# Two transformer-like blocks on one core: opening loads, the token factor of the feed-forward, buffers of the pooled branch, the sums at block two's entry, and a pause of VectorE

## The reference, cut to what matters

```python
h = rmsnorm(x, norm_mix)
q, k, v, r, lr_f, lr_b, u, g_a, g_b = split(h @ w_in)
log_a = log_sigmoid(lr @ w_decay_up + b_decay) / 16      # forward and backward, from 16 columns each
o = gla(q, k, v, log_a_f) + flipped gla(..., log_a_b)    # gated linear attention, 4 heads, chunks of 64
y_a = (rmsnorm(o) * gla_norm * silu(r)) @ w_branch_gla
y_b = pooled(u) @ w_pool_group * pool_scale              # 4 groups of 128 channels
x = x + (sigmoid(g_a) * y_a + sigmoid(g_b) * y_b) @ w_out
gate, up = split(rmsnorm(x, norm_ffn) @ w_ffn_in)        # 2816 columns each
x = x + (silu(gate) * up) @ w_ffn_out
x = rmsnorm(x, norm_final)
```

## Time and profile before

| what | us |
|---|---|
| device time, median of 3 runs (1457.41 to 1459.94) | 1459.5 |
| the profiled execution | 1460.08 |
| its span, first to last instruction | 1458.3 |
| TensorE (PE) busy | 1385.7 |
| VectorE (DVE) busy | 761.8 |
| ScalarE (ACT) busy | 575.7 |
| GpSimd (POOL) busy | 556.3 |

### The profile page before, as it was taken

The page is one execution under the profiler, slowest core; times in us unless marked ns, Lnnn a source line. Parts: engine busy times, 40 slices in busy tenths (PEclk is TensorE's granted clock), DMA queues, the critical chain, the costliest instruction groups (busy, mean ns, idle before and its releaser), DMA issues.

```text
span 1458.3 us, 18620 instructions
## 1 busy us (share of the span) xinstructions
PE 1385.7 (95%) x6812; PEld 1143.9 (78%) x6812; DVE 761.8 (52%) x1223; ACT 575.7 (39%) x777; POOL 556.3 (38%) x126
## 2 busy tenths in 40 slices
PE   7899999998997999999999799997999999999997
PEld 4688888876885888888888577766888888887886
DVE  3641451655737878877521352235777777302453
ACT  6443453442334222223222445554445554334233
POOL 4232323323343434433434233224444455434341
PEclk8999999998998999999999999998999999999998
DMA  6122212223323445545333242322222211232221
GB/s 189 55 87 87 80 50 74 85 73 116 115 87 100 131 131 154 147 130 152 96 99 98 59 130 86 101 58 58 58 58 58 58 58 58 61 113 86 87 87 58
DMA packets 201599, 133.68 MB, mean 92 GB/s; under 512 B 3479, under 2 KB 197768, under 8 KB 201558
## 3 DMA queue, kind: packets, MB, share of 16 engines
q1 hardware_dynamic: 200390, 130.68, 30.5%
q10 hardware_dynamic: 848, 1.60, 0.3%
q0 software_dynamic: 320, 0.84, 0.2%
HBM read 130.99 MB, written 2.12 MB: 91 GB/s over the span
## 4 chain that ended last, share of the span: by engine, by line
issue 68%; POOL 15%; PE 14%; ACT 1%; DMA 1%; POOLq 0%; SPq 0%; ACTq 0%; DVE 0%
POOL wlo L426 15%; PE acc L441 4%; PE acc L443 3%; PE acc L442 3%; PE acc L1723 1%; DMA raw<-in_w_in_dram 1%; PE acc L1725 1%; PE acc L1724 1%; PE mid L2091 0%; ACT hhi L669 0%; PE mid L2150 0%; ACT whi L422 0%; POOLq L1696 0%; SPq L528 0%; POOL masks L1690 0%
## 5 line engine op out<-in xcount | busy, mean ns | idle before, releaser
L426 POOL TENSOR_TENSOR wlo<-raw,whi 128x2048 fp32r<-128x2048 f32 (+2 forms) x112 | 550.0, 4911 | 873.3 <-ACT whi L422 873.3
L441 PE MATMUL acc<-hhi,whi 128*128 128x512 f32 x1152 | 461.5, 401 | 18.0 <-POOL wlo L426 15.9
L442 PE MATMUL acc<-hlo,whi 128*128 128x512 f32 x1152 | 450.9, 391 | 0.0
L443 PE MATMUL acc<-hhi,wlo 128*128 128x512 f32 x1152 | 450.6, 391 | 0.0
L441 PEld LDWEIGHTS acc<-hhi,whi 128*128 128x128 f32 x1152 | 217.6, 189 | 71.2 <-POOL wlo L426 19.7
L442 PEld LDWEIGHTS acc<-hlo,whi 128*128 128x128 f32 x1152 | 217.7, 189 | 46.0 <-issue 2.9
L443 PEld LDWEIGHTS acc<-hhi,wlo 128*128 128x128 f32 x1152 | 217.4, 189 | 46.4
L422 ACT ACTIVATE whi<-raw 128x2048 fp32r<-128x2048 f32 (+2 forms) x112 | 205.7, 1836 | 58.9 <-PE acc L443 42.7
L1388 DVE TENSOR_TENSOR ada<-ada 128x512 f32<-128x512 f32 x24 | 109.1, 4545 | 0.8
L441 PE MATMUL acc<-ahi,whi 128*128 128x512 f32 x176 | 68.7, 390 | 0.0
L442 PE MATMUL acc<-alo,whi 128*128 128x512 f32 x176 | 68.5, 389 | 0.0
(11 more groups left out here) (353 smaller groups left out, 2019.1 us busy)
## 6 DMA issues: line engine op xcount, KB each, us to landing
raw<-in_w_in_dram SPq DMA_DIRECT2D x57, 512.0 KB
raw<-in_w_in_dram SPq DMA_DIRECT2D x26, 1024.0 KB
raw<-in_w_ffn_in_dram SPq DMA_DIRECT2D x44, 512.0 KB
ada<-in_w_ada_dram SPq DMA_DIRECT2D x24, 512.0 KB, 3.8
raw<-in_w_ffn_out_dram SPq DMA_DIRECT2D x16, 704.0 KB
raw<-in_w_out_dram SPq DMA_DIRECT2D x8, 1024.0 KB
xnat<-in_x_dram SPq DMA_DIRECT2D x8, 512.0 KB, 7.0
raw<-in_w_branch_gla_dram SPq DMA_DIRECT2D x4, 1024.0 KB
```

The costliest lines, as they stand in the source:

```text
L426: nc.gpsimd.tensor_tensor(wlo[:, slot, 0:n], raw[:, slot, 0:n], whi[:, slot, 0:n].bitcast(f32), ALU.subtract).then_inc(s_unit_lo, 1)
L441: nc.tensor.matmul(acc[bank][:, :], h, xh[:, k, :], start=(k == 0), stop=False)
L442: nc.tensor.matmul(acc[bank][:, :], h, xl[:, k, :], start=False, stop=False)
L443: last = nc.tensor.matmul(acc[bank][:, :], lo, xh[:, k, :], start=False, stop=(k == nk - 1))
```

## The change

Opening loads: the 32 low-rank columns are loaded alone into `wlr` and multiplied in full float32, without a split, as four strips of 32 output rows (one for each of four tiles of channels); `lrT` and `wup` have four copies of the 32 rows, so that the next product sums the strips. Unit 0 no longer exists, so units change slots up to `U_POOL`. The masks' load waits until x is there; the loads of `wup` are eight. ScalarE empties q and k of head 0 before gate step 6.

Late token factor: the feed-forward's input is x times `norm_ffn`, split inside the `w_out` loop, without the root. VectorE multiplies the gate's sums by `nrs` before the sigmoid, and every tile of `w_ffn_out` by `nrs` squared; the mean product stands behind the first unit.

Pooled branch: weights and o have buffers of their own (`pwraw`, `pwhi`, `pwlo`, `ohi`, `olo`), and all eight low parts of o stand before VectorE's evictions.

Block two's entry: the last tile's squares are no longer added by VectorE; TensorE adds them as further products of the means. The high parts come before the second root, the split of unit `U_ATT + 1` stands before the squares, and its low part is made by VectorE.

Recurrence: VectorE waits, between L1546 and the level products, for GpSimd's split of the unit.

```diff
@@ opening: SyncE, ScalarE, GpSimd, TensorE
-            load(0, 0, kview(w_in, C_LR, P), ncol=P)
+            sp.dma_start(wlr[:, :, :], kview(w_in, C_LR, LR)).then_inc(s_lr_in, 16)
...
-            split_hi(act, 0, 0, KT * P)
...
-            A(lrT[:, :], acc[b][0:2 * RANK, :], ACT.Copy).then_inc(s_acc_free[b], 1)
+            A(lrT[:, :], acc[b][:, :], ACT.Copy).then_inc(s_acc_free[b], 1)
...
                 if i == 6:
-                    split_hi(act, 3, 1)
+                    head_evict_qk(0)
+                    split_hi(act, 3, 0)
...
+            for c in range(P // LR):
+                pool.dma_start(wup[c * LR:c * LR + RANK, 0, :], inp["w_decay_up_fwd"][0]).then_inc(s_wup_in, 16)
+                pool.dma_start(wup[c * LR + RANK:(c + 1) * LR, 1, :], inp["w_decay_up_bwd"][0]).then_inc(s_wup_in, 16)
+            pool.wait_ge(s_x_in[TT - 1], 16)
             pool.dma_start(mask_src[:, :, :], inp["masks"]).then_inc(s_mask_src, 16)
...
-            split_lo(pool, 0, 0, KT * P)
...
-            for k in range(KT):
-                pe.wait_ge(s_norm_lo, k + 1)
-                ks = slice(k * P, (k + 1) * P)
-                mm(acc[b][:, :], whi[:, 0, ks], hhi[:, k, :], start=(k == 0), stop=False)
-                mm(acc[b][:, :], whi[:, 0, ks], hlo[:, k, :], start=False, stop=False)
-                last = mm(acc[b][:, :], wlo[:, 0, ks], hhi[:, k, :], start=False, stop=(k == KT - 1))
+            strips = P // LR
+            for m in range(KT // strips):
+                pe.wait_ge(s_norm_lo, (m + 1) * strips)
+                for h in (hhi, hlo):
+                    for c in range(strips):
+                        k = m * strips + c
+                        last = mm(acc[b][c * LR:(c + 1) * LR, :], wlr[:, k, :], h[:, k, :].bitcast(f32),
+                                  start=(m == 0 and h is hhi), stop=(m == 1 and h is hlo), skip_group_check=True)
@@ pooled branch: ScalarE, VectorE
+                    for k in range(KT):
+                        A(ohi[:, k, :], o_all[:, k, :], ACT.Copy).then_inc(s_o_hi, 1)
...
             for k in range(KT):
+                dve.wait_ge(s_o_hi, k + 1)
+                V.tensor_tensor(olo[:, k, :], o_all[:, k, :], ohi[:, k, :].bitcast(f32), ALU.subtract)\
+                    .then_inc(s_o_lo, 1)
+            for k in range(KT):
...
-                dve.wait_ge(s_o_hi, k + 1)
-                V.tensor_tensor(hlo[:, k, :], o_all[:, k, :], hhi[:, k, :].bitcast(f32), ALU.subtract)\
-                    .then_inc(s_o_lo, 1)
@@ feed-forward: ScalarE, VectorE
                     norm_square(0, k)
+                    A(hhi[:, k, :], xres[:, k, :], ACT.Copy, scale=vcol[:, R_NF + k:R_NF + k + 1])\
+                        .then_inc(s_norm_hi, 1)
...
                 norm_add(0, k)
+                dve.wait_ge(s_norm_hi, nth(1) + k + 1)
+                V.scalar_tensor_tensor(hlo[:, k, :], xres[:, k, :], vcol[:, R_NF + k:R_NF + k + 1],
+                                       hhi[:, k, :].bitcast(f32), ALU.mult, ALU.subtract).then_inc(s_norm_lo, 1)
...
+                    dve.wait_ge(s_norm_rs, 1)
+                    dve.wait_ge(s_acc_full, gfull)
+                    V.tensor_tensor(fsg[:, j, :], acc[bg][:, :], nrs[:, :], ALU.mult).then_inc(s_f_norm, 1)
                     dve.wait_ge(s_f_sig, i * 2 + j + 1)
                     V.tensor_tensor(fsg[:, j, :], fsg[:, j, :], acc[bg][:, :], ALU.mult)\
                         .then_inc(s_acc_free[bg], 1)
...
+                    V.tensor_tensor(y, acc[b][:, :], nrs[:, :], ALU.mult).then_inc(s_acc_free[b], 1)
...
-                    V.tensor_tensor(x, x, acc[b][:, :], ALU.add).then_inc(s_acc_free[b], 1)
+                    V.tensor_tensor(x, x, y, ALU.add).then_inc(s_f_x, 1)
@@ block two's entry: ScalarE, VectorE, TensorE
+            split_hi(act, U_ATT + 1, 1)
...
+            A(fsg[:, 1, :], xres[:, k, :], ACT.Square, scale=vcol[:, R_NFIN + k:R_NFIN + k + 1]).then_inc(s_mid_sq, 1)
...
+            A(fsg[:, 0, :], xres[:, k, :], ACT.Square, scale=math.sqrt(EPS)).then_inc(s_mid_sq, 1)
+            A(nsq[:, 0, :], xres[:, k, :], ACT.Square).then_inc(s_norm_sq, 1)
...
+            V.tensor_tensor(wlo[:, 1, :], raw[:, 1, :], whi[:, 1, :].bitcast(f32), ALU.subtract).then_inc(s_unit_lo, 1)
...
-                    mm(M[1][:, :], mean_dm[:, :], fsg[:, 0, :], start=True, stop=True).then_inc(s_mid_sum, 1)
-                    mm(M[3][:, :], mean_dm[:, :], faa[:, 0, :], start=True, stop=True).then_inc(s_norm_sum, 1)
+                    mm(M[1][:, :], mean_dm[:, :], faa[:, 1, :], start=True, stop=False)
+                    mm(M[3][:, :], mean_dm[:, :], faa[:, 0, :], start=True, stop=False)
+                    pe.wait_ge(s_mid_sq, KT + 1)
+                    mm(M[1][:, :], mean_dm[:, :], fsg[:, 1, :], start=False, stop=False)
+                    mm(M[1][:, :], mean_dm[:, :], fsg[:, 0, :], start=False, stop=True).then_inc(s_mid_sum, 1)
+                    pe.wait_ge(s_norm_sq, nth(1) + KT)
+                    mm(M[3][:, :], mean_dm[:, :], nsq[:, 0, :], start=False, stop=True).then_inc(s_norm_sum, 1)
@@ recurrence: VectorE
                 V.tensor_tensor(hkd[:, :], hkd[:, :], hk[:, :], ALU.mult).then_inc(s_h_op, 1)
+
+                dve.wait_ge(s_unit_lo, (g + 1) * 2 + (U_HG + 2))
                 for lev in range(LEVELS):
```

More of the change, by code:

```diff
@@ L388, in nth, with added @@
             return n * KT
+        def added(n):
+            return n * KT - (n == 2)
         def x_bank(k):
@@ L861, in _, with ffn_out @@
                     ffn_tile(i, j)
-            with act.Fori(0, 4) as i:
+            nc.scalar.preload_act_table_set(LN_EXP)
+            def ffn_out(i, last=False):
                 for j in range(4):
@@ L865, in _ @@
                     split_hi(act, v + i * 4, v % 2, FT // 2 * P if j < 3 else 16 * P, lin=first_tile(v - 1) + i * 4)
-                    if j % 2:
+                    if j % 2 and not (last and j == 3):
                         k = i * 2 + j // 2
-                        act.wait_ge(*moved(U_FOUT, j, 4, i))
+                        act.wait_ge(s_f_x, i * 4 + j + 1)
                         act.wait_ge(s_norm_acc, k + nth(1))
@@ L1893, in _ @@
             g = GLA_HEADS - 1
-            units(U_C, 1)
+            pe.wait_ge(s_unit_lo, U_C + 1)
+            for j in range(2):
+                tile(U_C, j, 0, j)
             gla_scores(g)
```

278 lines of the change are left out of this document (151 added, 127 removed).

## The result

The changed kernel takes 1420.7 us (median of 4, 1420.0 to 1421.4), the kernel before 1458.5 in the same session (median of 4, 1456.5 to 1459.9): ratio 0.9743, 95% interval 0.9731 to 0.9755. 37.8 us were gained where 42 to 43 had been forecast (1416.4), inside the range. The profiled executions took 1421.4 and 1460.1, their spans are 1419.3 and 1458.3.

A forecast was written before the change was run, and what follows sets the result against it. TensorE, busy for 95% of the span, was taken as the bound, so only its waits and half-clock stretches count. Savings 2.5 + 5.8 + 9.8 + 2.7 + 6.8 + 15.5 = 43.1 us, from 1459.5 to 1416.4; range 1404 to 1431.

The forecast's parts named there:

- Opening, 2.5: Low-rank products at the start: four strips at once, 6.8 us for 8.3, and a start 1.5 earlier; 2.5 us saved.
- rival (b): Opening: strips go two by two or the clock stays low throughout; 7 us lost, 1423 us; chance 0.12.
- Eviction of q and k, 5.8: Head 0: earlier copies remove TensorE's wait for gq and its slow stretch, 6.2 us; net 5.8 after later splits.
- Pooled branch, 9.8: Low parts of o before all evictions: idle 5.9 and 3.9 us of slow stretch go; 9.8 us saved.
- Feed-forward, 2.7: Late factor: 4.2 us saved in w_ffn_in at a cycle of 11.39 us, 1.5 lost in w_ffn_out; net 2.7.
- rival (a): Feed-forward cycle fits within TensorE's 11.13 us; 5.3 us more gained, 1411 us; chance 0.15.
- Entry, 6.8: Block two's entry: 2.3 us from a shorter chain, 2.8 from VectorE's low weights, 1.7 from a slow stretch; 6.8 saved.
- Recurrence, 15.5: VectorE's pause lets GpSimd split: 8.5 us from seven waits, 5.0 from the first, 2.0 from a slow stretch.
- (d): Recurrence: GpSimd's 11.79 us split is its own length, not a wait for ports; slower, 1472 us; chance 0.03.
- (e): Recurrence: GpSimd gets the ports at VectorE's next instruction, so the pause brings nothing; 15.5 us less, 1432; chance 0.02.
- (c): Recurrence: the pause only moves lateness, ob and copies hold up the scores in 8 heads; 1424 us; chance 0.08.
- probably goes: Recurrence, first head: the slow stretch, 2.5 us lost for 4.92 busy, was expected to go; 2.0 us saved.

The follow-up runs named there:

- experiment 11: Changed kernel with the edits of experiments 4 to 8 together, opening strip products waiting only for high parts, and ScalarE's fourth-unit split before the table load: 1401.1 us.
- experiment 12: Kernel of experiment 11 with VectorE emptying the first head's query bank, and one hf operation, ahead of the last attention output: 1401.8 us.
- Experiment 2: Changed kernel with q and k of head 0 emptied behind the table load and sigmoid again: 1426.4 us.
- experiment 3: Changed kernel with the low parts of o made between VectorE's evictions again, their own buffers kept: 1432.6 us.
- experiment 5: Changed kernel with VectorE's product with nrs ahead of the first halving of ada in the feed-forward loop, not in the first unit: 1418.6 us.
- experiment 7: Changed kernel with ScalarE's squares behind the next unit's split in w_ffn_out: 1418.2 us.
- experiment 4: Changed kernel with the low part of block two's second weight unit made by GpSimd again instead of VectorE: 1419.8 us.
- experiment 10: Kernel of experiment 4 with ScalarE's split of block two's second weight unit behind the three squares: 1424.5 us.
- Experiment 1: Changed kernel without VectorE's wait for GpSimd's split in the recurrence: 1432.4 us.
- experiment 6: Changed kernel with TensorE taking a unit's ada column between the two tiles of the next unit: 1421.8 us.
- experiment 8: Changed kernel with GpSimd's split of the recurrence's third unit begun only after the first head's level products: 1413.7 us.
- experiment 9: Changed kernel with the 16 low-rank products reordered, each strip's high and low product next to each other: 1420.7 us, one run.

## Why the prediction was nearly right

**Opening, 2.5.** Too small. The start did not move (17.67 and 17.74; 16.9 to 18.0 in other traces of the same opening); I had given it 1.5. That the wait for four low parts took what the missing split gave is only in part borne out: waiting for the high parts alone, experiments 11 and 12 began at 17.1 and 16.5. The timeline of TensorE, which answers to the earlier trace rows:

```profile
17.74 1.93 PE L1829 MATMUL acc<-hhi,wlr 128*32 128x512 f32 x8 [3.02 <-DVE hlo L1209]
...
21.88 1.04 PE L1829 MATMUL acc<-hlo,wlr 128*32 128x512 f32 x8
22.86 0.33 PE L1833 MATMUL mid<-ident,vrow 128*128 128x128 f32 x1
```

Eight passes of 512 (x8) take as long as two, 0.86 us in the last row before the next starts (21.02 to 21.88), so the strips do run four at once: rival (b) is out. The stage took 5.1 us for 8.3, and not the 6.8 that I summed at half clock throughout. What I did not count was the rest: before, the products behind it had a second slow stretch, from 30.32 to 37.15, all busy, which cost 3.4 us and which no trace of the changed kernel or of its edits has. Why it went was not tested. By the place of the next wait TensorE was 6.8 us ahead.

**Eviction of q and k, 5.8.** Too large. The 6.2 went, but TensorE, now ahead, ran into the split of the fourth unit, 2.44 us and a stretch of 3.41 (1.7), where I had put 0.4: left 2.1. I worked out lateness against the old arrival of TensorE and not against the one that my own first term gave. Experiment 2 shows that the two waits are coupled, experiment 11 that the second goes if ScalarE splits ahead of its table load. The two misses cancel, and 8.3 came out as 8.7. That is luck, and closer than the stage repeats itself: it differs by some 2.5 us from trace to trace.

**Pooled branch, 9.8.** 10.2 measured; experiment 3 puts the cause in the order.

**Feed-forward, 2.7.** The net is 1.7. The cycle from faa to faa was forecast at 11.39 and is 11.28 and 11.35 in turn, more than TensorE's 11.13. The stall in the second unit is 2.15 for 2.2, but it brings a stretch at half clock, 1.7, which I left out. On the other hand I let TensorE follow the longer cycle at once; it ran at 11.13 us a unit until the tenth and lost 2.1 us in the units after that, so `w_ffn_in` gained 5.6 and not 4.2. (My sum says 19 cycles from the first faa; its result, 696.9, is that of 20, and 20 they are.) A cycle above 11.13 refutes rival (a), and experiment 5 shows the chain. `w_ffn_out` was the term that I mis-sized: I put the added operation of 0.72 against a slack of 0.75 and called it even. It is 0.83 with its hand-over (from 2.04 us between a tile's end and the split to 2.87), in every second tile. And a miss of 0.1 us costs more than 0.1: the tile that finds its weights missing ends 0.4 to 0.5 us late, four times 7.91 or 8.01 us after the one before and not 7.48, and two more are late by 0.6 and 0.3. These six make about 2.7 of the 3.8 lost, and experiment 7 gives 2.7 back; the other 1.1 is the wait of 0.75 at the first split and the slower start behind it. I had 1.5 in all.

**Entry, 6.8.** 7.0, in part for a reason that I had wrong. I gave 2.8 us to the low part made by VectorE. Experiment 4 shows that it brings nothing where ScalarE splits early, experiment 10 that the order on ScalarE brings 3.9.

**Recurrence, 15.5.** Here the largest miss lies, 3.9. That the seven waits of 1.2 us go was right, and so was the place of the pause. Experiment 1 refutes rivals (d) and (e), and the list of waits, which has none in the seven later heads, refutes (c). The forecast was 8.5 for the seven waits, 5.0 for the first and 2.0 for the slow stretch. Measured were:

- The seven heads gain 10.7: a head took 34.6 us and takes 33.0, so a wait of 1.24 us, with the slower start behind it, had cost 1.57.
- The first wait gains 6.8: the split came 0.6 us late and not 2.3. That is not to its credit. TensorE came to it later, by the new stretch at half clock at 956.16, which costs 1.7. In experiments 3, 5 and 6, which leave the recurrence alone, this stretch is missing and the wait is 2.16, as forecast:

```profile
967.17 0.50 PE L460 MATMUL acc<-hhi,whi 128*128 128x512 f32 x1 [2.16 <-POOL wlo L438]
```

- The slow stretch of the first head, of which I wrote that it "probably goes", is the sentence that failed. I had followed one split through the pause and not the next one, which then stopped the level products for 4.8 us. The stretch stayed, and with TensorE busy for 9.66 of its 10.24 us, where before it was for 4.92, it cost 2.4 us more than before, instead of the 2.0 less that I counted.
- 1.75 us of a new wait, for hsc, came on top.

10.7 + 6.8 - 1.7 - 2.4 - 1.75 is 11.65, and the stage gained 11.6. Experiment 8 takes away the wait and the slow stretch, 6.5 us.

So the total is right to 4 us in 42, while two of its parts rest on steps that failed, and misses of either sign offset each other.

## What to carry to other kernels

A step that is moved or sped up changes when its neighbours meet: work out each further lateness from the arrival times that the earlier terms of the sum give, and follow the shared resource through its next use, not only through the one that is being mended. Where two engines share a way, the order of short operations around the long one decides, and here it was enough to move an operation (a product that reads a bank, a split ahead of squares), where giving work to another engine brought nothing (experiment 4). Waits in a chain can each look worthless to remove, as 5 and 6 here, and be worth their full size together. And before a difference of 1 or 2 us in one stage of one trace is given to an edit, look whether its stretches at half clock are the same.

## What the runs showed of the hardware

- Which of VectorE and GpSimd is held is not settled by who is first. A split of GpSimd that began amid VectorE's differences took 11.79 us, and one that began 1.5 us into the level products of the same kind took 4.69 and held VectorE's product for 4.83 (experiment 8's first fence). In the feed-forward GpSimd came in while VectorE's product of 1.22 us ran, and VectorE's next operation was held for 5.01. In both kinds the split began while VectorE was at work. What decides stays open; no run told these apart.
- The VectorE product that reads one operand from a bank of sums was not held: 0.69 us amid a split of GpSimd (experiment 5), where in the changed kernel the halving, with both operands on chip, took 5.01.
- Four products of 32 columns in full float32 ran at once, at four times the rate (eight passes in 0.86 us), and TensorE found the overlap also where two products for one strip followed each other (experiment 9, one run).
- The granted clock rose and fell with no change of the program at the same place: the first stretch at half clock began between 13.6 and 17.9 us and was 3.41 to 10.24 us long in kernels with the same opening. The wait of 2.15 us for hq, which all these kernels have but that of experiment 12, was followed by a stretch of 3.41 us in the changed kernel and in experiments 2, 4, 7 to 11, and by none in the kernel before and in experiments 1, 3, 5 and 6.
